# A two-block transformer on one core: weight ring split into three unit slots and two half slots, and the first panel's products reordered

## The reference, cut to what matters

```python
def first_block(...):
    for l in range(2):
        mod = (silu(c) @ w_ada[l] + b_ada[l]).reshape(B, 3, 3, 1024)
        x = x + 0.5 * gate(0) * _swiglu(norm_mod(x, 0), w_ffn_up[l, 0], w_ffn_down[l, 0])
        x = x + gate(1) * _mixer(norm_mod(x, 1), ...)
        x = x + 0.5 * gate(2) * _swiglu(norm_mod(x, 2), w_ffn_up[l, 1], w_ffn_down[l, 1])

def second_block(...):
    for l in range(2):
        mod = silu(c2) @ w_mod[l] + b_mod[l]
        x = x + gt1 * (mix(rmsnorm(x) * (1 + sc1) + sh1) @ w_out[l])
        x = x + gt2 * (silu(h @ w1) * (h @ w3)) @ w2
    return rmsnorm(x, g_final)
```

## Time and profile before

| | us |
|---|---|
| median of three runs | 1650.31 |
| the three runs | 1650.31, 1643.76, 1655.65 |
| the profiled execution, its time | 1645.32 |
| its span | 1643.5 |
| TensorE busy in it | 1584.7 |
| VectorE busy | 1311.0 |
| ScalarE busy | 914.1 |

### The profile page before, as it was taken

The page is one execution under the profiler, slowest core; times in us unless marked ns, Lnnn a source line. Parts: engine busy times, 40 slices in busy tenths (PEclk is TensorE's granted clock), DMA queues, the critical chain, the costliest instruction groups (busy, mean ns, idle before and its releaser), DMA issues. The chain is left out here.

```text
span 1643.5 us, 31908 instructions
## 1 busy us (share of the span) xinstructions
PE 1584.7 (96%) x13268; PEld 1562.5 (95%) x13268; DVE 1311.0 (80%) x2070; ACT 914.1 (56%) x1567; POOL 84.9 (5%) x123
## 2 busy tenths in 40 slices
PE   2999999999999999999999999999999999999998
PEld 2999998999999999998999999999999999999998
DVE  6688888788888888887788788878888878785753
ACT  5445468565545555468664545566544456564552
POOL 5000000010000000100120001001000110010000
PEclk8999999999999999999999999999999999999999
DMA  9788774358777688754378777424887863345571
GB/s 355 281 341 328 287 280 148 131 221 326 308 314 282 260 330 332 287 214 153 143 267 307 295 300 267 148 103 168 306 318 290 320 225 121 140 168 225 216 257 47
DMA packets 57136, 403.05 MB, mean 245 GB/s; under 512 B 6578, under 2 KB 6834, under 8 KB 9248
## 3 DMA queue, kind: packets, MB, share of 16 engines
q1 hardware_dynamic: 55424, 395.84, 63.4%
q0 software_dynamic: 1568, 5.17, 1.1%
HBM read 399.94 MB, written 1.05 MB: 244 GB/s over the span
## 5 line engine op out<-in xcount | busy, mean ns | idle before, releaser
L1614 DVE TENSOR_TENSOR WL<-ring,WH 128x1024 fp32r<-128x1024 f32 (+1 forms) x508 | 600.3, 1216 | 170.6 <-ACT WH L1150 169.7
L515 PE MATMUL PS<-HH,WH 128*128 128x256 f32 (+1 forms) x2640 | 632.9, 282 | 14.7 <-ACT WH L1150 9.7
L515 PE MATMUL PS<-HL,WH 128*128 128x256 f32 (+1 forms) x2640 | 622.7, 279 | 0.0
L1150 ACT ACTIVATE WH<-ring 128x1024 fp32r<-128x1024 f32 (+1 forms) x508 | 511.0, 1049 | 103.1 <-DMA ring<-in_down 45.5
L515 PEld LDWEIGHTS PS<-HH,WH 128*128 128x128 f32 x2640 | 495.2, 189 | 18.5 <-ACT WH L1150 9.9
L515 PEld LDWEIGHTS PS<-HL,WH 128*128 128x128 f32 x2640 | 493.5, 189 | 0.6
L515 PE MATMUL PS<-HH,WL 128*128 128x256 f32 (+1 forms) x2640 | 374.0, 279 | 3.7 <-DVE WL L1614 3.6
L515 PEld LDWEIGHTS PS<-HH,WL 128*128 128x128 f32 x2640 | 336.4, 189 | 5.2 <-DVE WL L1614 5.2
L1641 DVE CUSTOM_DVE_ANT_0 ring<-ring,CB,VC 128x1024 f32<-128x1024 f32 x240 | 317.6, 1338 | 10.2 <-DMA ring<-in_ada 10.1
L515 PE MATMUL PS<-AH,WL 128*128 128x256 f32 x1056 | 294.8, 279 | 0.2 <-DVE WL L1614 0.2
L515 PE MATMUL PS<-AH,WH 128*128 128x256 f32 x1056 | 294.8, 279 | 0.0
(11 more groups left out here) (210 smaller groups left out, 1438.6 us busy)
## 6 DMA issues: line engine op xcount, KB each, us to landing
ring<-in_up SPq DMA_DIRECT2D x88, 1024.0 KB, 5.9
ring<-in_ada SPq DMA_DIRECT2D x72, 1024.0 KB, 7.2
ring<-in_ffn SPq DMA_DIRECT2D x66, 1024.0 KB, 5.5
ring<-in_mod SPq DMA_DIRECT2D x48, 1024.0 KB, 6.8
ring<-in_down SPq DMA_DIRECT2D x44, 1024.0 KB, 6.3
ring<-in_win SPq DMA_DIRECT2D x32, 1024.0 KB, 7.0
ring<-in_wout SPq DMA_DIRECT2D x16, 1024.0 KB, 4.8
ring<-in_winv SPq DMA_DIRECT2D x4, 1024.0 KB, 4.8
```

The source lines that it names most:

```text
L515: return e.matmul(out, lhsT, rhs, start=start, stop=stop, skip_group_check=skip)
L1150: e.activation(half_of(i)[0], slot_of(("unit", u))[:, w * (i % 2):w * (i % 2) + w], ACT.Copy).then_inc(s_hi, 1)
L1614: return e.tensor_tensor(out, a, b, op)
```

## The change

**The ring.** Slots 0 to 2 now hold units alone, unit i in slot i % 3. Slot 3 is cut in two half slots, one for the first and one for the second half of a modulation load, each with a semaphore of its own (s_ada). The eight modulation loads of the start still pass through four whole slots. SyncE now walks a list in the order in which VectorE uses things up (`used_up`): unit i+3 is issued when both remainders of unit i are made, and half j of modulation load i+1 when half j of load i is summed (a new semaphore s_modh tells of the first halves). So there are 224 half loads of 512 KB (rows of 4 KB out of rows of 8 KB) in place of 112 loads of 1 MB. `ADA_AT` is written otherwise, for the same ticks as before.

**The first panel.** For n > 0, `cols(..., first=True)` waits for s_lo first, and then makes, for each k from 0 to 7, the product WH by HH and the product WL by HH, after a wait for chunk k. The eight products WH by HL follow as before. The first sublayer's panel is unchanged.

The names `unit_landed`, `unit_at`, `ada_landed`, `ada_at` replace `landed` and `slot_of` in `hi_half`, `lo_half` and `ada_half`; nothing else moves on any engine.

```diff
-        loads = [("ada", (i + 4) % 8) for i in range(FIRST_ADA)] + [("unit", 0)]
+        used_up = [("unit", 0, 0)]
         for n in range(NSUB):
             for t in range(NTICK[SUBS[n][0]]):
                 if UNIT0[n] + t + 1 < len(units):
-                    loads.append(("unit", UNIT0[n] + t + 1))
-                loads += [("ada", i) for i, j in ada_halves(n, t) if j == 0]
-        place = {load: p for p, load in enumerate(loads)}
+                    used_up.append(("unit", UNIT0[n] + t + 1, 0))
+                used_up += [("ada", i, j) for i, j in ada_halves(n, t)]
...
+            for i in range(3):
+                e.wait_ge(s_mod, 4 + i + 1)
+                load_unit(i)
+            e.wait_ge(s_mod, 8)
+            load_half(FIRST_ADA, 0)
+            load_half(FIRST_ADA, 1)
+            for v, (kind, i, j) in enumerate(used_up):
+                if kind == "unit":
+                    if i + 3 < len(units):
+                        e.wait_ge(s_lo, 2 * i + 2)
+                        load_unit(i + 3)
+                elif i + 1 < NADA:
+                    e.wait_ge(*((s_modh, i - FIRST_ADA + 1) if j == 0 else (s_mod, i + 1)))
+                    if (i, j) == (71, 1):
+                        spread_c(1)
+                    load_half(i + 1, j)
...
                 if first:
-                    for ks in (range(KD - 1), (KD - 1,)) if n > 0 else (range(KD),):
-                        for k in ks:
-                            e.wait_ge(s_hh, 8 * n + k + 1)
-                            mm(out, wh[:, k, :], HH[:, k, 0:S], start=k == 0, stop=False)
+                    if n > 0:
                         e.wait_ge(s_lo, i + 1)
-                        for k in ks:
+                    for k in range(KD):
+                        e.wait_ge(s_hh, 8 * n + k + 1)
+                        mm(out, wh[:, k, :], HH[:, k, 0:S], start=k == 0, stop=False)
+                        if n > 0:
+                            mm(out, wl[:, k, :], HH[:, k, 0:S], start=False, stop=False)
+                    if n == 0:
+                        e.wait_ge(s_lo, i + 1)
+                        for k in range(KD):
                             mm(out, wl[:, k, :], HH[:, k, 0:S], start=False, stop=False)
...
             def ada_half(i, j):
-                if j == 0:
-                    if i == 72:
-                        e.wait_ge(s_cb, 2)
-                    e.wait_ge(*landed(("ada", i)))
+                if (i, j) == (72, 0):
+                    e.wait_ge(s_cb, 2)
+                e.wait_ge(*ada_landed(i, j))
...
+                elif i >= FIRST_ADA:
+                    ins.then_inc(s_modh, 1)
```

More of the change, by code:

```diff
@@ L71 @@
 OUT0 = {1: 0, 4: 4, 6: 8, 8: 16}
-ADA_AT = (9, 10, 11, 12)
+ADA_AT = {"mix1": (9, 9, 10, 10, 11, 11), "mix2": (9, 9, 10, 10, 11, 11)}
 def ada_halves(n, t):
@@ L83, in ada_halves @@
     else:
-        at = [q for q in halves if ADA_AT[q // 2] == t]
+        at = [q for q in halves if ADA_AT[SUBS[n][0]][q] == t]
     return [(first + q // 2, q % 2) for q in at]
@@ L127, in build @@
         s_slot = [sem(f"s_slot{i}") for i in range(NSLOT)]
+        s_ada = [sem(f"s_ada{j}") for j in range(2)]
         s_const, s_const_rest, s_vec, s_xload = sem("s_const"), sem("s_const_rest"), sem("s_vec"), sem("s_xload")
@@ L132, in build @@
         s_hi, s_lo, s_half = sem("s_hi"), sem("s_lo"), sem("s_half")
-        s_cload, s_cb, s_mod, s_shift = sem("s_cload"), sem("s_cb"), sem("s_mod"), sem("s_shift")
+        s_cload, s_cb, s_mod, s_shift, s_modh = (sem("s_" + k) for k in ("cload", "cb", "mod", "shift", "modh"))
         s_astep, s_dstep = sem("s_astep"), sem("s_dstep")
@@ L213, in build, with unit_landed, unit_at, ada_landed @@
                 if UNIT0[n] + t + 1 < len(units):
-                    loads.append(("unit", UNIT0[n] + t + 1))
-                loads += [("ada", i) for i, j in ada_halves(n, t) if j == 0]
-        place = {load: p for p, load in enumerate(loads)}
+                    used_up.append(("unit", UNIT0[n] + t + 1, 0))
+                used_up += [("ada", i, j) for i, j in ada_halves(n, t)]
         def ada_source(i):
             return (f"ada{i // 36}", i % 36) if i < 72 else (f"mod{(i - 72) // 24}", (i - 72) % 24)
[L221 to L226, removed]
+        def unit_landed(i):
+            return s_slot[i % 3], 16 * (2 + i // 3 + 1)
+        def unit_at(i):
+            return ring[:, i % 3, :]
+        def ada_landed(i, j):
+            return (s_slot[i % 4], 16 * ((i + 4) % 8 // 4 + 1)) if i < FIRST_ADA else (s_ada[j], 16 * (i - FIRST_ADA + 1))
+        def ada_at(i, j):
+            return ring[:, i % 4 if i < FIRST_ADA else 3, D * j:D * j + D]
         def half_of(i):
@@ L315, in build @@
         rs0, rs1 = SM_[:, 0:2], SM_[:, 2:4]
-        def first_rank(i):
-            return (i + 4) % 8 if i < FIRST_ADA else i
         def softmax_of(t):
@@ L397, in _, with load_unit, load_half @@
             spread_c(0)
[L398 to L413, removed]
+            def load_unit(i):
+                source, n = units[i]
+                e.dma_start(unit_at(i)[:, 0:2 * n], source).then_inc(s_slot[i % 3], 16)
+            def load_half(i, j):
+                name, k = ada_source(i)
+                e.dma_start(ada_at(i, j), A[name][k][:, D * j:D * j + D]).then_inc(s_ada[j], 16)
+            for p in range(FIRST_ADA):
+                i = (p + 4) % 8
+                if p >= 4:
+                    e.wait_ge(s_mod, p - 3)
+                name, k = ada_source(i)
+                e.dma_start(ring[:, p % 4, :], A[name][k]).then_inc(s_slot[p % 4], 16)
                 if p == 2:
                     e.dma_start(x_rows, A["x"].rearrange("(t p) d -> p t d", p=128)).then_inc(s_xload, 16)
-                if p == 14:
+            for i in range(3):
[14 more added lines that the diff above has]
+                    load_half(i + 1, j)
+                if v == 3:
                     e.dma_start(CN[:, 0:FIRST], A["consts"][:, 0:FIRST]).then_inc(s_const_rest, 16)
@@ L1146, in hi_half @@
                 w = units[u][1]
-                e.wait_ge(*landed(("unit", u)))
+                e.wait_ge(*unit_landed(u))
                 if i >= NSPLIT:
                     e.wait_ge(s_half, i - NSPLIT + 1)
-                e.activation(half_of(i)[0], slot_of(("unit", u))[:, w * (i % 2):w * (i % 2) + w], ACT.Copy).then_inc(s_hi, 1)
+                e.activation(half_of(i)[0], unit_at(u)[:, w * (i % 2):w * (i % 2) + w], ACT.Copy).then_inc(s_hi, 1)
             def hi(u):
@@ L1626, in lo_half @@
                 e.wait_ge(s_hi, i + 1)
-                tt(wl, slot_of(("unit", u))[:, w * (i % 2):w * (i % 2) + w], wh.bitcast(F32), ALU.subtract).then_inc(s_lo, 1)
+                tt(wl, unit_at(u)[:, w * (i % 2):w * (i % 2) + w], wh.bitcast(F32), ALU.subtract).then_inc(s_lo, 1)
             def lo(u):
@@ L1633, in ada_half @@
             def ada_half(i, j):
-                if j == 0:
-                    if i == 72:
-                        e.wait_ge(s_cb, 2)
-                    e.wait_ge(*landed(("ada", i)))
+                if (i, j) == (72, 0):
+                    e.wait_ge(s_cb, 2)
+                e.wait_ge(*ada_landed(i, j))
                 bias = vec(f"bada{i // 36}", 2 * (i % 36) + j) if i < 72 else vec(f"bmod{(i - 72) // 24}", 2 * ((i - 72) % 24) + j)
-                w = slot_of(("ada", i))[:, D * j:D * j + D]
+                w = ada_at(i, j)
                 ins = e.tensor_tensor_reduce(out=w, in0=w, in1=CB[:, :], scale=1.0, scalar=bias, op0=ALU.mult, op1=ALU.add,
```

## The result

The changed kernel takes 1670.3 us (median of four runs, 1668.7 to 1683.1) against 1649.9 us before: ratio 1.0144 over all runs, with a 95% interval of 1.0107 to 1.0181 (the medians alone give 1.0123, a loss of 20.3 us). That is slower by 1.4%, outside my range, and of my cases it is "half loads too late", to which I gave 0.04.

What follows compares the result with a forecast made beforehand. TensorE's own work, busy 96%, was taken as the bound. Gains of 1.9 us (ring) and 0.8 us (first panel), nothing for added loads, made 2.7 us off the median of 1650.3: forecast 1647.5 us, range 1632 to 1662.

Steps and rivals of the forecast that it cites:

- half loads too late: Rival: modulation halves take 7.2 us to land, two slots fall behind in sublayers 0 and 7; 1670 us, chance 0.04.
- the gap inside: First panels: TensorE's short wait for chunk 6 or 7 of HH, 0.08 to 0.18 us each, goes; 0.8 us in all.
- as before: End of the first panel: HL for k = 7 would still come late, unchanged by the new order.
- The ring, what it adds: Cost of 112 more load issues and two half slots for VectorE's modulation sums: put at nothing.
- the two slots keep up on average: Modulation half slots: a half lands in 5.9 us, under the 6.5 us that sublayer 0's demand leaves.
- 1.8 us at most: VectorE's longest wait for a modulation half, where two uses of a slot are only one tick apart.
- so it catches up in some ticks: VectorE absorbs its waits for halves in its idle time, 0.7 us a tick around 400 us.
- I take nothing: Size put on the half loads' added cost to TensorE; low end nothing, high end left to a rival.
- My limit of 6.5 us: Longest load time of a modulation half at which two half slots keep up with sublayer 0's 42 halves.
- one or two halves of 2.7 us in hand: TensorE's stock of work while VectorE's remainder is late, said to cover VectorE's waits for modulation halves.
- -1.9 us for the ring: Gain from earlier unit loads: four TensorE waits that hang on ScalarE's unit waits go; bounds nothing to 5.9 us.
- slow throughout: Rival: without the first panel's wait TensorE stays in the slow cadence in the later SwiGLU sublayers; 1659.0 us, chance 0.23.

Runs made afterwards that it cites:

- experiment 5: Kernel before (old ring, old panel) with each modulation load after the eighth issued as two half loads into its one slot; 1651.6 us, ratio 1.0047.
- experiment 3: Changed kernel with the same 4 MB cut as two unit slots and four half slots; 1648.7 us, ratio 1.0011 to the kernel before.
- experiment 2: Kernel before (old ring) with only the paired order of the first panel; 1637.9 us over ten runs, ratio 0.9945.
- panel alone: Old ring with the new paired first panel, run twice: 1637.9 us (ratio 0.9945), then 1639.3 us (ratio 0.9968).
- joint ring: Changed kernel with one ring of eight half slots for units and modulation, in VectorE's order of use, paired panel; 1630.0 us, again 1628.3 us.
- experiment 4: Changed kernel with each half load bringing only 128 of 1024 columns, the sums made from them thrown away; 1650.1 us, ratio 1.0031.

## Why the prediction was wrong

**What held.** TensorE is the bound. The unit loads three ticks ahead end ScalarE's waits. The modulation halves land in 5.9 us in the median, the very figure that I had worked out. In the panels of sublayers 2, 3 and 5 to 9 the gap inside is gone (no two starts over 0.125 us apart), and the early remainder costs nothing. In the two mixers of the first block the gap has only moved: the step ahead of the last chunk of HL grew to 0.32 us, from 0.22 and 0.16 before, which I had not foreseen ("as before").

**The step that failed** is in "The ring, what it adds": "the two slots keep up on average", "1.8 us at most", "so it catches up in some ticks", and "I take nothing". The mechanism with its place stood there as a rival, and what was wrong was the use of a median where the coincidences decide. I traced each half from issue to landing: nothing in flight ahead of it, 3.5 us (median of 10); one unit, 5.4 us (61 halves); one unit and the other half, 5.6 us (92 halves), 8.7 at most; two units and the other half, 7.1 us (57 halves), 8.6 at most. And the half that is wanted soonest is issued right beside a unit load, since VectorE frees both within a tick. My limit of 6.5 us compared the median with an average demand; 76 of the 224 halves lie over it. VectorE waited for 47 of these and for 19 below it: 66 waits, 115 us. The largest of them was 3.8 us, not 1.8. The page of the kernel after has the halves and their medians:

```profile
ring<-in_ada SPq DMA_DIRECT2D x128, 512.0 KB, 5.9
ring<-in_mod SPq DMA_DIRECT2D x96, 512.0 KB, 5.9
```

**The cover.** I gave TensorE "one or two halves of 2.7 us in hand". The chain at 1256 us shows a wait of 3.79 us giving a stop of 1.94, so the cover was under 2 us there. VectorE's idle time did help, as I had said, only not enough. It is mostly its wait for WH, and this shrank, first before and then after:

```profile
DVE WL L1614 <- ACT WH L1150: 169.7, 162, 5.7
```
```profile
DVE WL L1637 <- ACT WH L1173: 93.6, 116, 5.6
```

So of the 115 us of new waits 76 were taken out of this idle time, and TensorE's waits for WL grew by 28. The 0.7 us a tick is an average, and one wait of 2 or 3 us is more than it can take up.

**The sum.** Instead of -1.9 us for the ring it was +28 us in waits for WL and +3 us of clock: the term "what it adds", put at nothing, was the one that failed. The "late halves" rival was given 23 us, close to the 20 measured, and a chance of 0.04 because half the bytes seemed to settle it. That its 1670 us came out is in part luck: it was worked out from halves that all take 7.2 us, and their median was 5.9 in sublayer 0 too, where it put 16 of its 23 us. Half the bytes do not settle it: the landing time of a half is mostly what stands ahead of it. The bytes and the number of loads before it should have been added up from the timeline of SyncE, for the tick with two halves.

**The cadence.** Its size (6.6 us for a sublayer) and its part in the spread fit the account. My rival "slow throughout", 0.23, was wrong in sign: a panel without a gap begins fast more often, not always slow. The row that I read for it, 118 ns in the first products, says nothing of where the pace ends: in the kernel after the panels begin at 118 ns as well, and every one of the seven goes on at 113.3.

**The page cited.** In the Trainium skill, "DMA: Bandwidth & Descriptors" (section "Anatomy of one DMA") fits loads issued by GpSimd with 2.0 us plus their bytes over 436 GB/s, which makes an estimated 3.2 us for a half load. The halves here are issued by SyncE and took 3.5 us (median of 10) with nothing ahead, so the rule is near for an idle queue; it says nothing of the 7.1 us behind two units. Its section "Bandwidth" advises batches of 1 MiB or more, which is half borne out: half rows cost 5.8 us in the old ring (experiment 5), but the fastest kernel of this study loads everything by halves.

## What to carry to other kernels

When a shared ring is split by kind of load, count for each kind the time from "used up" to "wanted again" at its shortest, and set it against the landing time with everything ahead that can be ahead, not against the median. Depth belongs to the loads that the engine with less slack waits for: VectorE, 80% busy, passed on 28 of 115 us of waits, while ScalarE, 56% busy, waited over 80 us for loads in the kernel before and TensorE felt 2 us of it. The same memory as two unit slots and four half slots took back about two thirds of the loss, and one ring in the order of use, with the paired panel, was faster than both kernels. Compare each variant with the one that differs in one thing alone: against the kernel before, experiment 3 seemed free, and against experiment 2 it costs 11 us. Before a difference of under 1% is explained in a kernel bound by TensorE, count products per window: between two profiles of the panel alone the cadence differs by 12 us, and the runs of the kernel before spread over 20 us in one round.

## What I had not expected of the hardware

TensorE runs the same stream of 256-column products at 113.3 or at 117.8 ns each, at a granted clock of 1.00 in both; it keeps a cadence for up to some 1550 products at a time (sublayer 0 of the joint ring), and which one it takes differs between executions of one program. Within SwiGLU sublayers it mostly changes at a short wait, but in experiment 4 it changed four times at the start of a down projection without any. Eleven executions of the joint ring fall in two groups, six at 1626.5 to 1628.3 and five at 1632.6 to 1634.8 us, and 6.6 us, the price of one slow sublayer, is about the step between them. The six runs of the first round, on another chip, fall in the same two groups (1626.6 to 1627.8 and 1632.3 to 1634.6), and the two profiles bear it out: that of the first round is in the upper group (1632.3) and has sublayer 5 in the slow cadence from near its start, and that of the second is in the lower (1627.1) and has no SwiGLU sublayer so.
